# DeltaNet heads: decay rows broadcast from memory, key lengths from the Gram diagonal, one product for the output's squares, and no last state

## The chip, the cores and the metric

The kernel runs on one core of one Trainium2 chip. Such a core has five engines that run side by side and meet at semaphores: TensorE (PE in the profile, with PEld for its weight loads), VectorE (DVE), ScalarE (ACT), GpSimd (POOL) and SyncE (SP), which here only issues DMAs. The metric is the device time of one execution in microseconds. The kernel before took 3912.97 us (median of 3 runs, 3911.88 to 3916.1).

## The reference

The program is a network of four layers on 512 tokens of width 1024, with a context of 256 tokens. The change touches one mixer, the bidirectional gated DeltaNet. For each of 8 heads of width 128, and for each of two directions:

```
q, k, v = silu(conv3(h @ w_in));  q = l2norm(q) * 128**-0.5;  k = l2norm(k)
beta = sigmoid(...);  g = -exp(a_log) * softplus(... + dt_bias)
gc    = cumsum(g) within a chunk
decay = exp(gc_i - gc_j) for j <= i, else 0
L     = tril(beta * k k^T * decay, -1)
[u|w] = solve(I + L, [beta v | beta exp(gc) k])
per chunk:  v_new = u - w @ S
            o     = (q exp(gc)) @ S + (q k^T * decay) @ v_new
            S     = S * exp(gc_last) + (k exp(gc_last - gc))^T @ v_new
out = (o_forward + o_backward) * rsqrt(mean(o^2) + 1e-6) * onorm * silu(z)
```

The context (2 chunks of 128 tokens here) is scanned first and gives no output; its last state starts the scan of the 4 latent chunks. The state after the last chunk is used by nothing.

## The kernel before, in words

The stage `DeltaHeads` (class at L2133) does the heads one after another. Tokens are cut in `NTA` = 6 chunks of 128 (two of context, four latent). `l` is the direction, 0 forward and 1 backward. Each engine runs an order written out by hand, in `tensor`, `scalar`, `vector`, `gpsimd` and `sync`; semaphores with one count per head (`PER`, `COUNTED`) join them. A head has two parts:

- The inverse (`tensor_invert`, `scalar_invert`, `vector_invert`) builds (I + L)^-1 in levels v = 1 to 6. Per level and direction, PE multiplies (`masked`, L2498), DVE masks the product (L2838), PE adds it in (`update`, L2517 and L2519), and DVE transposes the sum for the next level (L2844, L2848) while ACT copies it (L2698). PE's small products of 64 rows go between: the values turned after v = 1, the keys turned in v = 3.
- The scan (`tensor_scan` and the others) walks 6 steps of both directions. Per step: `z` (L2554), the right side `r` on DVE (L2874), `vn` (L2568), copied by ACT (L2742), the output's two products (L2582, L2586), the state's product (L2591) and its update on DVE (L2893). Between these PE projects the next head's q, k, v and gate (`three`, L588, products of rounded float32), and DVE and ACT convolve and activate them.

What the change touches:

- Decay rows. `decays` (L2402) makes each direction's row of gc, repeated over the 128 partitions, by 6 products of a broadcast column with a triangle of ones, into PSUM banks 6 and 7. ACT's `decay` (L2635) reads it: 6 Relu, an exponential of those, and an exponential of the row itself. For head h+1, direction 0's products stand in level 5 of head h's inverse and direction 1's behind step 0 of its scan.
- Key lengths. `gram` (L2416) makes k k^T per chunk in step 3, and then, from squares that ACT took of k (`square_k`), 6 products with a column of ones (L2427). DVE's `column_scales` (L2765) takes those sums at the end of step 3.
- Output norm. In the next head's inverse: ACT squares o (`square_o`), PE sums in 8 products of one column (`tensor_sums`, L2457 and L2458, behind level 3), ACT takes the root (`deviate_o`), DVE inverts it (`invert_root`, in level 4), PE spreads it over the partitions in 4 products (`tensor_spread`, L2465, behind level 4), and DVE multiplies (`norm_o`, L2829).
- The last step of a scan makes a state that nobody reads (L2884, L2591, L2893).

The weights of the next head are four DMAs on SP, issued when the last projection of the head before is done; ACT rounds them (`weight_high`, in levels 1 to 4) and POOL makes their low parts (`weights_low`, L582).

Of the kernel before, what the change touches and what calls it, by code (L numbers as in the profile page):

```python
# [27 lines left out]
P = 128  # L28
# [1923 lines left out]
G_MIX = G_LANE + 2 * LANE  # L1952
LEVELS = 7
# [3 lines left out]
class DeltaGates:  # L1957
# [3 lines left out]
    def __init__(self, core):  # L1961
        self.c = core
        self.n = core.slab(k_slab(core.d["w_in_a_2"][0], 4 * D, 4 * D + 32))
        self.rows, self.rows0 = core.shared("table_in", 48)
# [168 lines left out]
class DeltaHeads(Stage):  # L2133
# [13 lines left out]
    PER = {"slab": 64, "full": 6, "centre": 5, "conv": 5, "silu": 6, "square": 1, "coef": 1, "nk": 1,  # L2147
           "osq": 1, "ostd": 1, "oroot": 1, "weighed": 1, "mixed": 1, "values_out": 1, "keys_out": 1, "qk": 1,
           "tri": 2, "cross": 2, "side": 1, "scored": 1, "a": 12, "a_in": 10, "a_out": 14, "x": 12,
           "upd": 12, "z": 10, "r": 10, "vn": 12, "vn_out": 13, "vnd": 12, "su": 12, "s": 12, "o": 1,  # L2150
           "begun": 7, "grew": 5, "onorm": 2}


    COUNTED = {"rows": ("begun", (1, 2)), "gram": ("begun", (3,)), "lens": ("begun", (4,)), "qkp": ("begun", (5,)),
               "turned": ("begun", (6, 7)), "flat": ("grew", (1, 3)), "grown": ("grew", (2, 4)), "eg": ("grew", (5,)),
               "osum": ("onorm", (1,)), "ospread": ("onorm", (2,))}

    def __init__(self, core, gates):
# [11 lines left out]
        self.sums, self.inverse, self.nk, self.root = (v(G_COL + 72 + 6 * i, n) for i, n in enumerate((NTA, NTA, NTA, NT)))  # L2170
# [33 lines left out]
    def gpsimd(self, pool):  # L2204
        for h in range(DHEADS):
            if h == 0:
                self.weights_low(pool, 0)
            self.halve_decays(pool, h)
            self.pool_head(pool, h)
            if h + 1 < DHEADS:  # L2210
                self.weights_low(pool, h + 1)
        self.weigh_o(pool, DHEADS - 1)
# [9 lines left out]
    def pool_head(self, pool, h):  # L2222

        if h:
            self.wait(pool, h - 1, "o", 1)
            self.wait(pool, h - 1, "s", 12)
# [12 lines left out]
        if h:  # L2239
            self.weigh_o(pool, h - 1)  # L2240

# [57 lines left out]
    def sync(self, sp):  # L2299
# [15 lines left out]
    def tensor(self, pe):  # L2315
        self.project(pe, 0, 1, range(KD))
# [5 lines left out]
        self.decays(pe, 0, 0)  # L2322
        self.decays(pe, 0, 1)
# [6 lines left out]
        self.tensor_spread(pe, DHEADS - 1)  # L2330

    def vector(self, dve):
# [18 lines left out]
        for h in range(DHEADS):  # L2351
            self.vector_invert(dve, h)
            self.vector_scan(dve, h)
        self.invert_root(dve, DHEADS - 1)
        self.norm_o(dve, DHEADS - 1)

    def scalar(self, act):
# [8 lines left out]
        self.square_k(act, 0)  # L2366
        self.centre(act, 0, 4)
        self.silu(act, 0, 3)
        self.silu(act, 0, 4)
        self.gate(act, 0)  # L2370
# [31 lines left out]
    def decays(self, pe, h, l):  # L2402

        c = self.c
        if l == 1:
            self.wait(pe, h, "grown", 1)
        elif h:
            self.wait(pe, h - 1, "keys_out", 1)
        else:
            pe.wait_ge(self.cols, 1)  # L2410
        for t in range(NTA):
            ins = pe.matmul(c.pair(6, KEYS)[:, P * t:P * t + P], self.g_all[:, t, l, h:h + 1].to_broadcast([P, P]),
                            c.const(("cum_f", "cum_b")[l]), start=True, stop=True)
        ins.then_inc(self.s["begun"], 1)

    def gram(self, pe, h):  # L2416
# [3 lines left out]
        self.wait(pe, h, "grown", 2)  # L2420
# [3 lines left out]
        ins.then_inc(self.s["begun"], 1)  # L2424
        self.wait(pe, h, "square", 1)
        for t in range(NTA):
            ins = pe.matmul(c.ps[:, 7, TC + t:TC + t + 1], self.lane(0, L_L, NTA, P)[:, t, :],  # L2427
                            c.const("ones")[:, 0:1], start=True, stop=True)
# [22 lines left out]
    def tensor_sums(self, pe, h):  # L2451

        c = self.c
        self.wait(pe, h, "osq", 1)
        for t in range(NT):
            out, cols = c.ps[:, 5, TC + t:TC + t + 1], slice(P * t, P * t + P)
            pe.matmul(out, self.o_sq[:, cols], c.const("one_over_p")[:, 0:1], start=True, stop=False)  # L2457
            ins = pe.matmul(out, self.q_sq[:, cols], c.eps(4), start=False, stop=True)  # L2458
        ins.then_inc(self.s["onorm"], 1)

    def tensor_spread(self, pe, h):
        c = self.c
        self.wait(pe, h, "oroot", 1)
        for t in range(NT):
            ins = pe.matmul(c.ps[:, 5, P * t:P * t + P], self.root[:, t:t + 1].to_broadcast([P, P]),  # L2465
                            c.const("ident"), start=True, stop=True)
        ins.then_inc(self.s["onorm"], 1)

    def tensor_invert(self, pe, h):
# [13 lines left out]
        def masked(v, l):  # L2483
# [5 lines left out]
            elif h and l == 0:  # L2489
                self.wait(pe, h - 1, "s", 12)  # L2490
# [38 lines left out]
        for v in range(2, LEVELS):  # L2529
# [4 lines left out]
            if v == 5 and h + 1 < DHEADS:  # L2534
                self.decays(pe, h + 1, 0)
# [4 lines left out]
            if v == 4 and h:  # L2540
                self.tensor_spread(pe, h - 1)

    def tensor_scan(self, pe, h):
        c, s = self.c, self.s
        more = h + 1 < DHEADS
        for step in range(NTA):
# [27 lines left out]
            for l in range(2):  # L2574
# [13 lines left out]
                self.wait(pe, h, "vnd", i + 1)  # L2588
                if i == 0:
                    self.wait(pe, h, "keys_out", 1)  # L2590
                pe.matmul(c.ps[:, 2 * l, 2 * P:3 * P], self.kt[:, t, :], self.st(l, 3), start=True, stop=True)\  # L2591
                    .then_inc(s["su"], 1)
            if more:
                self.project(pe, h + 1, step, range(5, KD))
                if step == 0:
# [1297 lines left out]
```

## Time and profile before

| | |
|---|---|
| runs before, median (lowest, highest) | 3912.97 us (3911.88, 3916.1) |
| the profiled execution | 3914.16 us |
| its span | 3912.3 us |
| PE busy | 3454.4 us, 88% |
| DVE busy | 1812.2 us, 46% |
| ACT busy | 1110.1 us, 28% |
| POOL busy | 420.5 us, 11% |

The profiled execution's time holds its span and 1.9 us around it. The busy share of an engine is an average over all stages; what an instruction is worth is read in its own stage, from the timeline. A row of the timeline gives a start, how long the merged group lasted, its line and its tiles; a bracket behind it gives the engine's idle time before it and who ended it. One float32 product shows as two matmul records.

### The profile page before, as it was taken

Reading aid. Unit: us, or ns where it says so; the run is one execution under the profiler, and the core shown is the slowest. Engines: PE = TensorE matmul, PEld = TensorE weight load, DVE = VectorE, ACT = ScalarE, POOL = GpSimd, SP = SyncE. Lnnn points to the kernel's source line nnn. Section 1 sums busy time; section 2 is a strip of 40 time slices with the busy share of each in tenths; the row PEclk is TensorE's granted clock in tenths of the full one; section 3 lists DMA queues with packets and bytes.
Section 4 is the critical chain, followed back from the end, with each engine's and each line's share of the span. In section 5 each row is a group of like instructions: output and inputs, shape, how many; then the busy total and the mean of one; then the engine's idle time right before and its main releaser. Section 6 shows DMA issues by size and latency. Waiting matters only on the chain. (4 is left out here: it accounts for less than half of the span.)

```text
span 3912.3 us, 48632 instructions
## 1 busy us (share of the span) xinstructions
PE 3454.4 (88%) x18766; PEld 2323.2 (59%) x18766; DVE 1812.2 (46%) x2892; ACT 1110.1 (28%) x1849; POOL 420.5 (11%) x420
## 2 busy tenths in 40 slices
PE   8999899878999899887999998699987896998886
PEld 6756577754756677755888887444332674443332
DVE  6773777447865777435455445411111543111112
ACT  3051433223201433235544453211111322111112
POOL 1200000000300000002222320011111000111110
PEclk7999999988999899998999998799999897999998
DMA  6430355320622255310001001299997413999995
GB/s 220 172 109 22 107 173 172 114 108 22 247 108 86 86 172 172 109 26 23 23 23 45 23 23 46 98 414 392 424 415 300 167 45 118 417 402 415 398 391 218
DMA packets 222472, 689.48 MB, mean 176 GB/s; under 512 B 27699, under 2 KB 107699, under 8 KB 197076
## 3 DMA queue, kind: packets, MB, share of 16 engines
q1 hardware_dynamic: 192000, 648.17, 43.2%
q10 hardware_dynamic: 11572, 21.96, 1.5%
q0 software_dynamic: 18720, 16.84, 1.3%
q8 instruction: 126, 2.06, 0.2%
q14 instruction: 54, 0.44, 0.0%
HBM read 697.38 MB, written 40.89 MB: 189 GB/s over the span
## 5 line engine op out<-in xcount | busy, mean ns | idle before, releaser
L588 PE MATMUL psum<-work_rounded 128*128 128x512 f32 (+1 forms) x2224 | 815.4, 407 | 80.3 <-DVE work_rounded L582 30.3
L588 PE MATMUL psum<-work_rounded,ring_rounded 128*128 128x512 f32 (+1 forms) x1824 | 726.1, 398 | 0.0
L588 PEld LDWEIGHTS psum<-work_rounded 128*128 128x128 f32 x2224 | 428.7, 193 | 203.0 <-issue 93.9
L3434 PE MATMUL psum<-ring,fixed 128*64 128x512 f32 x1184 | 415.8, 657 | 96.1 <-DMA ring<-in_w 52.9
L577 ACT ACTIVATE work_rounded<-ring 128x1024 fp32r<-128x1024 f32 x204 | 214.6, 1057 | 950.7 <-PE psum L588 692.7
L588 PE MATMUL psum<-fixed_rounded,work_rounded 128*128 128x512 f32 (+1 forms) x1088 | 435.9, 401 | 0.0
L588 PEld LDWEIGHTS psum<-work_rounded,ring_rounded 128*128 128x128 f32 x1824 | 352.6, 193 | 81.1
L3589 DVE TENSOR_TENSOR work<-work,psum 64x512 f32<-64x512 f32 (+1 forms) x64 | 44.2, 691 | 701.9 <-ACT work L3519 547.3
L582 DVE TENSOR_TENSOR ring_rounded<-ring,work_rounded 128x1024 fp32r<-128x1024 f32 x189 | 230.1, 1220 | 283.0 <-ACT work_rounded L577 283.0
L3434 PEld LDWEIGHTS psum<-ring,fixed 128*64 128x64 f32 x1184 | 131.7, 150 | 333.0 <-issue 333.0
L362 DVE SCALAR_TENSOR_TENSOR work<-ring,fixed,work 128x512 f32<-128x512 f32 x364 | 300.5, 835 | 24.8 <-issue 0.9
L3434 PE MATMUL psum<-work,fixed 128*64 128x512 f32 x512 | 240.8, 626 | 0.0
L588 PE MATMUL psum<-ring_rounded 128*128 128x512 f32 (+1 forms) x768 | 238.5, 372 | 0.3 <-issue 0.3
L588 PEld LDWEIGHTS psum<-fixed_rounded,work_rounded 128*128 128x128 f32 x1088 | 210.7, 194 | 46.6 <-issue 2.6
L1274 DVE SCALAR_TENSOR_TENSOR work<-psum,fixed,work 128x511 f32<-128x511 f32 (+1 forms) x152 | 109.4, 720 | 142.1 <-ACT work L1356 108.2
L3519 ACT ACTIVATE work<-psum 64x512 f32<-64x512 f32 x53 | 31.3, 590 | 477.5 <-PE psum L3434 477.5
L3422 PE MATMUL psum<-ring,fixed 128*128 128x512 f32 x352 | 158.9, 611 | 1.8 <-DVE fixed L3581 1.8
L3343 POOL DMA_INDIRECT pair_rows<-work x66 | 66.7, 1011 | 809.0 <-DVE work L3605 663.8
L582 POOL TENSOR_TENSOR ring_rounded<-ring,ring_rounded 128x1024 fp32r<-128x1024 f32 x32 | 76.7, 2410 | 715.8 <-ACT ring_rounded L577 715.8
L588 PEld LDWEIGHTS psum<-ring_rounded 128*128 128x128 f32 x768 | 139.2, 189 | 21.1 <-issue 1.6
L582 POOL TENSOR_TENSOR ring_rounded<-ring,fixed_rounded 128x1024 fp32r<-128x1024 f32 x23 | 48.6, 2115 | 873.3 <-ACT fixed_rounded L577 873.3
L588 PE MATMUL psum<-fixed_rounded,ring_rounded 128*128 128x512 f32 (+1 forms) x384 | 137.0, 357 | 0.0
(396 smaller groups left out, 5159.7 us busy)
## 6 DMA issues: line engine op xcount, KB each, us to landing
ring<-in_w SPq DMA_DIRECT2D x128, 2048.0 KB, 17.3
work<-in_w SPq DMA_DIRECT2D x64, 2048.0 KB, 21.5
ring<-in_mod_w SPq DMA_DIRECT2D x24, 2048.0 KB, 9.0
ring<-in_ada_w SPq DMA_DIRECT2D x24, 2048.0 KB, 7.9
ring<-in_ffn_w_in SPq DMA_DIRECT2D x44, 1024.0 KB, 7.6
ring<-in_ffn_w_out SPq DMA_DIRECT2D x10, 2048.0 KB, 7.7
ring<-in_w_in_a SPq DMA_DIRECT2D x32, 512.0 KB, 6.6
ring<-in_hy_w_in SPq DMA_DIRECT2D x6, 2048.0 KB, 8.2
```

The costliest lines, as they stand in the source:

```text
L362: ins = dve.scalar_tensor_tensor(out=acc, in0=w[:, k, :], scalar=c.par(cond, k), in1=acc, op0=ALU.mult, op1=ALU.add)
L577: return act.activation(c.rounded(out), v, ACT.Copy)
L582: return eng.tensor_tensor(c.rounded(v), v, c.rounded(v_high), ALU.subtract)
L588: ins = pe.matmul(out, c.rounded(w), c.rounded(x), start=(start and i == 0), stop=(stop and i == 2))
L1274: dve.scalar_tensor_tensor(out=out[:, 1:n], in0=u[:, 0:n - 1], scalar=w0, in1=out[:, 1:n], op0=ALU.mult, op1=ALU.add)
L3343: pool.indirect_dma_start(self.c.d["pair_rows"], bass.IndirectOffsetOnAxis(ap=self.si[:, b:b + 1].bitcast(U32), axis=0), self.y_sb[:, b, : ...
L3422: ins = pe.matmul(c.ps[:, 2 + j, :], self.gt_sb[:, k, :], weights(o, j)[:, k, :], start=(k == 0), stop=(k == KD - 1))
L3434: ins = pe.matmul(c.ps[64 * j:64 * j + 64, 2, :], self.gt_sb[:, k, 0:64], weights(o, j)[:, k, :], start=(k == 0), stop=(k == KD - 1))
L3519: act.activation(self.s_sb[64:P, :].rearrange("p (k q) -> p k q", k=4), by_row(c.ps[0:64, 2, :]), ACT.Silu)\
L3589: dve.tensor_tensor(hh, s_sb, by_row(c.ps[rows, bank, :]), ALU.mult).then_inc(self.prod, 1)
```

## The change

- `decays` and its products go. Once, before head 0, PE transposes the table of all gc (96 columns) and ACT copies it out and writes it to DRAM (`keep_table`). SP then loads each direction's row, repeated over 128 partitions (`load_rows`, 384 KB), into one buffer in SBUF: direction 1 of a head when ACT is done with direction 0 (`grown` 1), direction 0 of the next head when it is done with direction 1 (`grown` 2). SP's weight DMAs of a head stand ahead of its direction 1. `decay` reads the buffer.
- `square_k` and the 6 products with ones go. `column_scales` multiplies the Gram product by the identity's halves and reduces.
- `square_q` takes a scale, POOL adds it to the squared output (`add_q`, ahead of its other work on a head), and one product of 512 columns sums and repeats it. DVE transposes the result (`turn_o`, in level 4), ACT takes the root of every 32nd column after its copies of level 4, and DVE inverts and spreads by a transposition (`invert_root`, now in level 5). `tensor_spread` goes.
- The last step makes no new state.

```
     def sync(self, sp):
...
+        def load_rows(h, l):
+            rows = self.table.rearrange("(t l) (b n) -> l b t n", l=2, n=P)[l, h]
+            sp.dma_start(self.rows_sb, rows.partition_broadcast(P)).then_inc(self.s["rows"], 16)
+
         for h in range(DHEADS):
             if h:
                 self.wait(sp, h - 1, "full", 6)
...
+            if h == 0:
+                sp.wait_ge(self.gates.rows, self.gates.rows0 + 64)
+                load_rows(0, 0)
+            self.wait(sp, h, "grown", 1)
+            load_rows(h, 1)
+            if h + 1 < DHEADS:
+                self.wait(sp, h, "grown", 2)
+                load_rows(h + 1, 0)
...
     def pool_head(self, pool, h):
         if h:
+            self.add_q(pool, h - 1)
             self.wait(pool, h - 1, "o", 1)
...
+    def add_q(self, pool, h):
+        self.wait(pool, h, "osq", 1)
+        pool.tensor_tensor(self.o_sq, self.o_sq, self.q_sq, ALU.add).then_inc(self.s["ofull"], 1)
...
     def tensor(self, pe):
-        self.decays(pe, 0, 0)
-        self.decays(pe, 0, 1)
+        pe.wait_ge(self.cols, 1)
+        pe.transpose(c.ps[0:96, 6, 0:P], c.view(G_GC, 96), c.const("ident")).then_inc(self.gates.turned, 1)
...
     def gram(self, pe, h):
-        self.wait(pe, h, "square", 1)
-        for t in range(NTA):
-            ins = pe.matmul(c.ps[:, 7, TC + t:TC + t + 1], self.lane(0, L_L, NTA, P)[:, t, :],
-                            c.const("ones")[:, 0:1], start=True, stop=True)
...
     def tensor_sums(self, pe, h):
+        self.wait(pe, h, "ofull", 1)
+        pe.matmul(c.ps[:, 5, :], c.const("one_over_p"), self.o_sq, start=True, stop=True).then_inc(self.s["osum"], 1)
...
     def tensor_scan(self, pe, h):
-                self.wait(pe, h, "vnd", i + 1)
                 if i == 0:
                     self.wait(pe, h, "keys_out", 1)
-                pe.matmul(c.ps[:, 2 * l, 2 * P:3 * P], self.kt[:, t, :], self.st(l, 3), start=True, stop=True)\
-                    .then_inc(s["su"], 1)
+                if step < NTA - 1:
+                    self.wait(pe, h, "vnd", i + 1)
+                    pe.matmul(c.ps[:, 2 * l, 2 * P:3 * P], self.kt[:, t, :], self.st(l, 3), start=True, stop=True)\
+                        .then_inc(s["su"], 1)
...
+    def keep_table(self, act):
+        act.wait_ge(self.gates.turned, 3)
+        act.activation(self.rows_sb[0:96, 0, :], self.c.ps[0:96, 6, 0:P], ACT.Copy).then_inc(self.cols, 1)
+        act.wait_ge(self.cols, 2)
+        act.dma_start(self.table.rearrange("a (b n) -> (a b) n", n=P), self.rows_sb[0:96, 0, :]).then_inc(self.gates.rows, 16)
...
     def column_scales(self, dve, h):
+        for half in self.halves():
+            dve.tensor_tensor(diagonal[half], g[half, :, half], self.ident()[half], ALU.mult)
+        dve.drain()
+        dve.tensor_reduce(self.sums, diagonal, AX.X, ALU.add)
+        dve.drain()
...
     def vector_invert(self, dve, h):
                 self.cross(dve, h, v - 1)
+            if v == 4 and h:
+                self.turn_o(dve, h - 1)
+            if v == WHOLE and h:
+                self.invert_root(dve, h - 1)
             for l in range(2):
                 turn(v, l)
```

The order of the instructions, before and now, at three places. PE, head 1's inverse, from the end of the sums (L2457, L2458) over levels 4 and 5, before:

```order
L2457 MATMUL psum<-fixed,work 128x1
L2458 MATMUL psum<-fixed,work 128x1
L2498 MATMUL psum<-work 64x64 x24
L2519 MATMUL psum<-work 64x64 x24
L2465 MATMUL psum<-fixed,work 128x128 x4
L2498 MATMUL psum<-work 64x64 x24
L2412 MATMUL psum<-fixed,work 128x128 x6
L2517 MATMUL psum<-work 64x64
```

The spread (L2465) and the next head's decay rows (L2412) stand between the levels' own products. The same place now (L2490 is `masked`, L2509 and L2511 `update`, L2459 the new sum):

```order
L2511 MATMUL psum<-work 64x64 x24
L2459 MATMUL psum<-work,fixed 128x512
L2490 MATMUL psum<-work 64x64 x24
L2511 MATMUL psum<-work 64x64 x24
L2490 MATMUL psum<-work 64x64 x24
L2509 MATMUL psum<-work 64x64
```

One product of 512 columns stands where eight of one column stood, and nothing between levels 4 and 5 or within level 5. DVE, levels 4 and 5 of the same inverse, before (L2838 masks, L2844 transposes):

```order
L2818 TENSOR_SCALAR work<-work 128x12
L2838 TENSOR_TENSOR work<-psum,work 128x384 x2
L2844 STREAM_TRANSPOSE work<-psum 128x384 x2
L2822 RECIPROCAL work<-work 128x4
L2838 TENSOR_TENSOR work<-psum,work 128x384 x2
L2848 TENSOR_TENSOR work<-work,psum 64x384 x2
```

Now (the lines of the mask and the level's transposition have moved, the names of the tiles tell them):

```order
L2813 TENSOR_SCALAR work<-work 128x12
L2839 TENSOR_TENSOR work<-psum,work 128x384 x2
L2817 STREAM_TRANSPOSE work<-psum 128x512
L2845 STREAM_TRANSPOSE work<-psum 128x384 x2
L2839 TENSOR_TENSOR work<-psum,work 128x384 x2
L2822 RECIPROCAL work<-work 128x16
L428 STREAM_TRANSPOSE work<-work 128x512
L2849 TENSOR_TENSOR work<-work,psum 64x384 x2
```

A transposition of 512 columns (L2817) has come in ahead of level 4's own, and the reciprocal with a spread (L428) ahead of level 5's last addition. DVE, the end of step 3 of head 0's scan and the start of step 4, before:

```order
L2893 SCALAR_TENSOR_TENSOR work<-work,psum 128x128 x2
L2768 TENSOR_SCALAR work<-psum 128x6
L2770 RECIPROCAL work<-work 128x6
L2772 TENSOR_TENSOR work<-work 128x12
L2782 TENSOR_TENSOR work<-work,psum 64x384 x2
L2874 SCALAR_TENSOR_TENSOR work<-psum,work 128x128 x2
```

Now (L2900 is the state's update, L2877 the right side of step 4):

```order
L2900 SCALAR_TENSOR_TENSOR work<-work,psum 128x128 x2
L2759 TENSOR_TENSOR work<-psum,work 64x384 x2
L2761 TENSOR_REDUCE work<-work 128x6
L2763 TENSOR_SCALAR work<-work 128x6
L2765 RECIPROCAL work<-work 128x6
L2767 TENSOR_TENSOR work<-work 128x12
L2777 TENSOR_TENSOR work<-work,psum 64x384 x2
L2877 SCALAR_TENSOR_TENSOR work<-psum,work 128x128 x2
```

Three instructions of up to 384 columns have come in between the state of step 3 and the right side of step 4.

## Rows read from the trace of the kernel before

**Rows 1.** All heads: us, busy (x) of PE, PEld, DVE, ACT, POOL; clock, DMA share, GB/s

```profile
1838.00:2426.00 588.00, 556.99 (x6965) 494.51 (x6966) 298.45 (x689) 272.76 (x578) 148.83 (x99) 0.98 0.11 30
```

**Rows 2.** Timeline of TensorE: start, us, engine, line, operation, records, idle before

```profile
1926.61 0.38 PE L2457 MATMUL psum<-fixed,work 128*128 128x1 f32 x2
...
1932.45 1.16 PE L2465 MATMUL psum<-fixed,work 128*128 128x128 f32 x8 [0.77 <-DVEq L2823]
...
1933.54 1.61 PE L2498 MATMUL psum<-work 64*64 64x64 f32 x48
...
1935.09 1.60 PE L2412 MATMUL psum<-fixed,work 128*128 128x128 f32 x12
...
1949.57 1.60 PE L2412 MATMUL psum<-fixed,work 128*128 128x128 f32 x12 [0.29 <-ACT work L2645]
...
1951.01 0.61 PE L2554 MATMUL psum<-work 128*128 128x128 f32 x4
```

**Rows 3.** The same timeline, TensorE, later steps of head 1's scan

```profile
1960.46 0.39 PE L2586 MATMUL psum<-work 128*128 128x128 f32 x2
...
1966.62 1.40 PE L2427 MATMUL psum<-fixed,work 128*128 128x1 f32 x12
...
1973.30 0.75 PE L2568 MATMUL psum<-work 128*128 128x128 f32 x4
...
1988.56 0.86 PE L2480 MATMUL psum<-work,fixed 64*64 64x384 f32 x4 [0.26 <-DVEq L2798]
```

**Rows 4.** Timelines of ACT, DVE and TensorE, last projection to first inverse

```profile
1813.36 0.60 ACT L2623 ACTIVATE work<-psum 128x512 f32<-128x512 f32 x1 [1.98 <-PE psum L588]
...
1833.35 1.12 DVE L2782 TENSOR_TENSOR work<-work,psum 64x384 f32<-64x384 f32 x2
...
1838.08 1.55 PE L2480 MATMUL psum<-work,fixed 64*64 64x384 f32 x4 [5.61 <-DVEq L2798]
```

**Rows 5.** Timeline of ACT, next head's decay work in the scan

```profile
1944.97 1.66 ACT L2641 ACTIVATE work<-psum,work 128x128 f32<-128x128 f32 x6
...
1948.72 0.79 ACT L2645 ACTIVATE work<-psum 128x768 f32<-128x768 f32 x1
...
1953.68 1.67 ACT L2641 ACTIVATE work<-psum,work 128x128 f32<-128x128 f32 x6
...
1956.85 0.21 ACT L2648 ACTIVATE work<-work 128x12 f32<-128x12 f32 x1
```

**Rows 6.** DMA issues over the whole span: count, KB each, median us to landing

```profile
ring<-in_w_in_a SPq DMA_DIRECT2D x32, 512.0 KB, 6.6
...
work<-in_masks ACTq DMA_DIRECT2D x1, 416.0 KB, 3.9
```

**Rows 7.** Timeline of DVE, steps 3 to 5 of the scan

```profile
1970.84 0.16 DVE L2768 TENSOR_SCALAR work<-psum 128x6 f32<-128x6 f32 x1
...
1971.70 1.12 DVE L2782 TENSOR_TENSOR work<-work,psum 64x384 f32<-64x384 f32 x2 [0.19 <-issue]
...
1972.89 0.61 DVE L2874 SCALAR_TENSOR_TENSOR work<-psum,work 128x128 f32<-128x128 f32 x2
...
1986.50 0.55 DVE L2793 TENSOR_TENSOR work<-work 128x384 f32<-128x384 f32 x1
```

**Rows 8.** Timelines of ACT and POOL: next head's first weights, and a triangle

```profile
1922.54 1.06 ACT L577 ACTIVATE ring_rounded<-ring 128x1024 fp32r<-128x1024 f32 x1 [1.53 <-DMA ring<-in_w_in_a]
...
1923.68 4.68 POOL L582 TENSOR_TENSOR ring_rounded<-ring,ring_rounded 128x1024 fp32r<-128x1024 f32 x2 [3.11 <-ACT ring_rounded L577]
...
1956.33 1.84 POOL L2220 TENSOR_TENSOR work<-work,fixed 128x768 f32<-128x768 f32 x1 [5.63 <-ACT work L2644]
```

**Rows 9.** Timeline of DVE, head 1's triangular inverse

```profile
1927.24 1.22 DVE L2815 COPY work<-work 128x6 f32<-128x6 f32 x2
...
1929.45 1.26 DVE L2838 TENSOR_TENSOR work<-psum,work 128x384 f32<-128x384 f32 x2 [0.85 <-PE psum L2498]
```

**Rows 10.** One line's instructions (L428, a spread over 512 columns): min/median/max ns

```profile
L428 DVE STREAM_TRANSPOSE work<-work x15: 445/711/712, 52.1 to 3902.7; 128x512 f32<-128x512 f32 x13, 128x256 f32<-128x256 f32 x2
```

More of the change, by code:

```diff
@@ L2169, in __init__ @@
         self.kd, self.gl, self.eg, self.bg, self.coef, self.ahead = (v(G_COL + 12 * i, 2, NTA) for i in range(6))
-        self.sums, self.inverse, self.nk, self.root = (v(G_COL + 72 + 6 * i, n) for i, n in enumerate((NTA, NTA, NTA, NT)))
+        self.sums, self.inverse, self.nk, self.root = (v(G_COL + 72 + 6 * i, n) for i, n in enumerate((NTA, NTA, NTA, T // 32)))
+        self.rows_sb = v(G_ROWS, NTA, P)
+        self.table = core.d["h_rows"][0:2 * NTA, :]
         self.taps = v(PAR0 + PAR["conv_a0"][0], 3, 3, DHEADS)
@@ L2419, in gram @@
         self.wait(pe, h, "silu", 2)
-        self.wait(pe, h, "grown", 2)
+        if h == 0:
+            pe.wait_ge(self.cols, 2)
         for t in range(NTA):
@@ L2629, in convolve @@
             .then_inc(self.s["conv"], 1)
-    def square_k(self, act, h):
-        act.drain()
-        act.activation(self.lane(0, L_L, KEYS), self.k, ACT.Square).then_inc(self.s["square"], 1)
+    def keep_table(self, act):
[3 more added lines that the diff above has]
+        act.dma_start(self.table.rearrange("a (b n) -> (a b) n", n=P), self.rows_sb[0:96, 0, :]).then_inc(self.gates.rows, 16)
     def decay(self, act, h, l):
         c, s = self.c, self.s
-        m, rows = self.lane(l, L_M, NTA, P), c.pair(6, KEYS).rearrange("p (t n) -> p t n", n=P)
-        self.wait(act, h, "rows", l + 1)
+        m, rows = self.lane(l, L_M, NTA, P), self.rows_sb
+        self.wait(act, h, "rows", 16 * l + 16)
         for t in range(NTA):
@@ L2685, in deviate_o @@
         c = self.c
-        self.wait(act, h, "osum", 1)
-        act.activation(self.root, c.ps[:, 5, TC:TC + NT], ACT.Sqrt, bias=c.eps(5)).then_inc(self.s["ostd"], 1)
+        self.wait(act, h, "oturn", 1)
+        act.activation(self.root, fine(self.o_sq), ACT.Sqrt, bias=c.eps(5)).then_inc(self.s["ostd"], 1)
     def scalar_invert(self, act, h):
@@ L2818, in scan_columns, with turn_o @@
         dve.tensor_scalar(self.bg, self.eg, -1.0, None, ALU.mult)
+    def turn_o(self, dve, h):
+        self.wait(dve, h, "osum", 1)
+        dve.transpose(self.o_sq, self.c.ps[:, 5, :])
+        dve.drain().then_inc(self.s["oturn"], 1)
     def invert_root(self, dve, h):
@@ L2822, in invert_root @@
         dve.reciprocal(self.root, self.root)
-        dve.drain().then_inc(self.s["oroot"], 1)
+        dve.drain()
+        spread(dve, self.o_sq, self.root)
+        dve.drain()
     def norm_o(self, dve, h):
-        self.wait(dve, h, "ospread", 1)
         self.wait(dve, h, "weighed", 1)
-        dve.scalar_tensor_tensor(out=self.mixed(h), in0=self.mixed(h), scalar=self.c.par("onorm_a"), in1=self.c.ps[:, 5, :],
+        dve.scalar_tensor_tensor(out=self.mixed(h), in0=self.mixed(h), scalar=self.c.par("onorm_a"), in1=self.o_sq,
                                  op0=ALU.mult, op1=ALU.mult).then_inc(self.s["mixed"], 1)
@@ L2890, in vector_scan @@
                 t = self.order[l][step]
+                if step == NTA - 1:
+                    continue
                 self.wait(dve, h, "su", i + 1)
```

77 lines of the change are left out of this document (24 added, 53 removed).

## The prediction

> **What bounds the kernel now.** I read the busy time over the eight heads first [rows 1]: in 588 us PE is busy for 557, 95%, at a granted clock of 0.98, while DVE has 298, ACT 273 and POOL 149. So PE's own order sets the pace, and an instruction taken out of it is worth its time, unless PE would then stand at a wait that it covered. The timeline of PE shows where those are. From the first product of head 0's inverse at 1838.08 to that of head 2 at 1988.56 [rows 3, 4] two heads take 150.5 us, and the later ones repeat head 1. Within a head PE idles 0.3 to 0.8 us at a few places only, each with a bracket. The reader is to look there for who is late, and at the start of the stage, where PE idled 5.61 us before the first inverse [rows 4]. Then I read DVE, ACT and POOL beside PE, for what they do in the moment when PE would come earlier.
>
> **Step 0 of the scan: 1.73 us less.** The second set of decay rows starts at 1949.57 after 0.29 us of idleness and the next product starts at 1951.01 [rows 2]. Both go: 1.44 + 0.29 = 1.73. The state it needs next has been ready since before.
>
> That holds if the row load is in time, and this is the step with a new wait. ACT has finished direction 0 at 1948.72 + 0.79 = 1949.51 [rows 5]; SP issues the load then, and ACT stands before direction 1 until it has landed. Queued behind are the rest of `decay`, the copies of step 2's `vn`, and with them PE's second output product of step 2 (L2586) and the state's product. From the start of direction 1 to the end of its work ACT needs 1956.85 + 0.21 - 1953.68 = 3.4 us, and the copy 0.4 more [rows 5]. PE now comes to L2586 at 1960.46 - 1.73 = 1958.7 [rows 3]. So the load has 1958.7 - 3.8 - 1949.5 = 5.4 us; I take 5.3, since the state's product needs a DVE step too. The load is 384 KB to 128 partitions in runs of 512 bytes. Nearest rows: 416 KB of masks landed in 3.9 us, issued last of three; 512 KB of weights, in the same runs, in 6.6, as one of four issued together [rows 6], so its figure holds the queueing. I take 4.0; ends 2.6 (a third below the masks, for a queue with nothing ahead) and 6.6. At 4.0 nothing waits; at 6.6 it is 1.3 us in each of 7 heads, 9 in all.
>
> By the Trainium skill, DMA: Bandwidth & Descriptors, section "Anatomy of one DMA", a DMA takes about 2.0 us plus its bytes over 436 GB/s, an estimate of 2.9 us here. By that rule the sum would be some 2 us better than mine at the start of the stage and no different in the scan. The masks' row is a microsecond above it, and I keep the row.
>
> **Steps 3 and 4: 0.5 us more.** The sums of the squared keys are 12 records from 1966.62 on, 1.40 us with the tail of the last, 1.3 of PE's time [rows 3]. They go. But their sums come back on DVE, in front of step 4's right side: two products of 64x384 like L2782 (1.12 for two), a reduction over 384 columns (about 0.55, as one of these), and drains between (0.1): 1.8 [rows 7]. Has DVE room? The right side starts at 1972.89 in two halves of 0.3, and PE starts the `vn` that reads it at 1973.30 [rows 3, 7]: no slack at all. So PE stands 1.8 where it saved 1.3. ACT's square of the keys goes too, beside other work, at nothing.
>
> **Step 5: 0.45 us less** on PE: two products of the state, 4 records, at 12 records in 1.44 us [rows 2] 0.48. DVE loses its two updates and could begin the next inverse about 1 us ahead of 1986.50 (the products' 0.5 and two halves of 0.3, as the like right side takes [rows 7]).
>
> The scan in total: 1.73 - 0.5 + 0.45 = 1.7 us a head.
>
> **The inverse to level 5: 2.2 us less.** Here PE loses 8 sums (16 records, about 1.9 us) and gets one product of 512 columns (0.9, as 8 records of 128 columns by the same 1.44 for 12), and loses the spread with its wait: 0.77 and then 1.1 until 1933.54 [rows 2]. The boundary before could give 1 us more, since DVE is late there. That would be some 4 us. I don't count so much, as DVE is next late, held by something that the change doesn't move. ACT waits for the weights of the next head until 1922.54, SP having issued them with the end of the projections; POOL's first two low parts run from 1923.68 to 1928.36 [rows 8]; and DVE's tiny copies of 6 columns (1.22 us for two, from 1927.24 [rows 9]) end only when POOL is done. They are tied to the landing of the weights, however early PE is. Now from there: DVE masks level 4 at once, from 1928.6 rather than 1929.45, for 1.26 us [rows 9]; then the new transposition of the output's sums, 0.71 by the spread of as many columns [rows 10], with a drain 0.8; it ends at 1930.7. Level 4's own first transposition, of 384 columns, follows, 0.6 by the same row, and PE begins level 5 at 1931.3 instead of 1933.54: 2.2 less. Without the new transposition it would be near 3. The bounds: 1.3 if DVE's waits grow by another such step, 4.0 if POOL does not hold DVE. ACT's root comes later than now but before DVE asks for it.
>
> POOL's new addition is 1.2 us long, half of a low part with twice its columns [rows 8], and it waits for ACT's square, which stands behind two ACT copies of its size (0.60 each [rows 4]). So all of POOL's work on the head comes about 3 us later, up to the point where it waits for the weights anyway; that gap, 3.11 us [rows 8], covers it. What reads that work (step 1 of the scan and later, the low parts) is 10 us off.
>
> The Trainium skill, SBUF — State Buffer, section "Who interferes with whom", says that a DVE instruction with two inputs in SBUF and a GpSimd instruction that reads SBUF keep each other out, and so do DVE copies in a fast mode. It speaks against the change, which gives POOL an addition and `norm_o` a second input in SBUF. The copies above agree with it; were POOL's low parts pushed later, DVE would be held longer, a microsecond a head, inside my bounds.
>
> **Level 5: 1.44 us less.** The first decay rows start at 1935.09 [rows 2] and their 12 records take 1.44 as in step 0; DVE's mask is ready by then. The reciprocal and the spread, about 1.0 with drains [rows 10], now stand ahead of DVE's last addition. Between DVE's mask and that addition PE has 36 records for one direction, 1.2 us at 48 in the 1.55 from 1933.54 on [rows 2], which hides them.
>
> **Head 0, head 7, start, tail.** Head 0 has no output before it: 1.7 + 1.4 = 3.1. Head 7 has no weights to follow, so nothing holds DVE: about 2.2 + 1.0, and 0.5 in its scan: 3.7, the tail costing 0.1 (POOL's addition, a transposition and a spread for eight sums, a PE spread and its wait). The start: ACT is at the last projection's result at 1813.36 [rows 4]. PE's transposition and ACT's copy 0.6, the write out 2.6 (the low end again, 48 KB), a load 4.0: ACT begins at 1820.6. Direction 0, with a table load, is 1949.51 - 1944.97 = 4.5; the second load 4.0; direction 1's first exponential is there 1956.85 - 1953.68 - 0.7 = 2.5 later, at 1831.6; POOL's triangle 1.84 [rows 5, 8]. So DVE begins its second weighing at 1833.4, where it began at 1833.35 before [rows 4], and the first inverse follows as before, at 1838.1. The long waits are paid by the Gram products, the lengths, the scores and the first weighing, which ran behind the decays and now run beside the loads. I take 0, at ends -5 (6.6 us a load) and +3.
>
> **Sum.** Six heads at 1.7 + 2.2 + 1.44 = 5.34: 32.0; with 3.1, 3.7 and 0: 38.8. Against the profiled execution (3914.2; its span 3912.3 and 1.9 around) it gives 3875.4; it stood 1.2 above the median of the runs, so 3874.
>
> **The rivals.**
> - The loads are slow, 6.6 us: 9 us in the scans and 5 at the start come back, 3888. For it: the same short runs as the weights; against: nothing is queued ahead. 15 in 100.
> - The cover is gone: PE's removed work stood where it would wait anyway, for ACT's or DVE's copies, in level 5 and in step 0 as well. Half of the sum, 3894. For it: a chain of three engines in each level; against: in level 5 and step 0 the records follow without a gap. 12 in 100.
> - POOL does not hold DVE: the inverse gives 4.0 rather than 2.2, 6 times 1.8 is 11: 3863. 13 in 100.
> - Slower: 128 partitions that all read the same 3 KB of memory are served one after another. Each us of a load beyond 5.3 costs 7 in the scans, each beyond 4.0 costs 2 at the start: 7 (x - 5.3) + 2 (x - 4.0) = 38.8 gives x = 9.3 us, from which on the change loses. At twice the weights' figure, 13.2 us, it is 55 + 18 = 73 against 39: 3947. The trace shows no load of this kind of that size. 6 in 100.
>
> **How the numbers follow.** The forecast of 3874, with an own range of 3866 to 3884, has 54 in 100. Within 0.2% (8 us, what a measurement of this kernel can't tell from no change) lies only what is left between the half sum and the slow loads. Faster 91, same 3, slower 6. The range takes in the first three cases: 3861 to 3895.
>
> **What would show it.** Right: ACT's first Relu of direction 1 waits for a DMA of about 4 us and L2586's successor doesn't wait for ACT; PE idles about 1.8 us before `vn` of step 4 for DVE; level 5 starts at 0.5 us of idleness behind level 4; the two heads of 150.5 us take 142 (3.1 and 5.3 less); PE's first inverse starts near 1838. Wrong: a load over 5.3 us, with PE waiting for ACT in step 2, the two heads over 147 us, or PE waiting for DVE's inverse where it did not before.

## The result, and the profile after

| | before | after |
|---|---|---|
| median (lowest, highest) | 3914.53 us (3911.88, 3916.28), on the same chip | 3954.74 us (3950.0, 3956.11) |
| after / before | | 1.0102 [1.0089, 1.0115] |
| the profiled execution, its span | 3914.16, 3912.3 | 3950.0, 3948.2 |
| first products of head 1 to head 7, a sixth | 76.33 | 79.67 |

The change makes the kernel slower by 1.0%, 40 us, where 39 us less were forecast. The heads of the profile after, and three stretches of head 1 (the columns are those of [rows 1]):

```profile
1848.00:2444.00 596.00, 510.64 (x6438) 443.99 (x6439) 313.23 (x674) 265.16 (x561) 156.05 (x107) 0.94 0.18 42
1971.90:1978.30 6.40, 0.20 (x2) 0.01 (x1) 0.00 (x0) 3.79 (x11) 1.01 (x1) 0.72 0.06 14
1978.30:1985.00 6.70, 6.56 (x20) 5.40 (x21) 2.51 (x6) 2.85 (x6) 0.80 (x1) 0.50 0.19 37
1985.00:1988.00 3.00, 3.00 (x28) 3.00 (x27) 1.37 (x5) 1.20 (x3) 0.00 (x0) 1.00 0.22 44
```

PE was busy for 557 of 588 us [rows 1]; now it is for 511 of 596. The work is gone, the time is not: PE stands. The next two stretches show where. For 6.4 us in the middle of the scan it does nothing, and for the 6.7 us after that it is busy, but at a granted clock of 0.50, its lower level of 1.2 GHz.

Who is late is read from the row loads: the DMA's issues, what the loads took from issue to landing, and the waits over the heads (total us, times, longest).

```profile
work<-h_rows SPq DMA_DIRECT2D x16, 384.0 KB, 11.1
...
h_rows<-work ACTq DMA_DIRECT2D x1, 48.0 KB, 1.5
```

```profile
DMA to landing us min/median/max: 10.9/11.1/12.5
```

```profile
ACT work L2630 <- DMA work<-h_rows: 78.4, 8, 12.6
...
PE psum L2574 <- ACT work L2733: 45.6, 7, 7.4
...
PE psum L2472 <- DVEq L2793: 37.8, 2, 37.5
...
PE psum L2490 <- DVE work L2845: 16.2, 22, 0.9
...
PE psum L2556 <- DVE work L2877: 11.8, 7, 1.7
```

A load takes 11.1 us in the median and never under 10.9, where 4.0 were taken. ACT stands for it before direction 1 of each head (L2630 is `decay`'s Relu), the copy of `vn` (L2733) stands behind it, and PE's second output product of step 2 (L2574, L2586 before) waits 45.6 us in seven heads. The timelines of PE and of ACT in head 1 show it as one event:

```profile
1971.72 0.38 PE L2570 MATMUL psum<-work 128*128 128x128 f32 x2
...
1978.37 0.80 PE L2574 MATMUL psum<-work 128*128 128x128 f32 x2 [6.26 <-ACT work L2733]
...
1984.95 0.63 PE L2542 MATMUL psum<-work 128*128 128x128 f32 x4
```

```profile
1974.44 1.86 ACT L2630 ACTIVATE work<-work 128x128 f32<-128x128 f32 x6 [9.15 <-DMA work<-h_rows]
...
1977.96 0.61 ACT L2733 ACTIVATE work<-psum,work 128x128 f32<-128x128 f32 x2
```

From L2574 to the next `z` (L2542) 6.58 us pass. The same instructions took 3.22 before, from 1960.46 [rows 3] to `z` at 1963.68. So the stall costs 6.3 us and the slower stretch behind it another 3.4. At the start of the stage two such loads follow each other, and the first inverse begins 40.6 us after PE ends its last projection (at 1807.91), where it was 24.8 (from 1813.32 to 1838.08):

```profile
1838.23 1.86 ACT L2630 ACTIVATE work<-work 128x128 f32<-128x128 f32 x6 [12.57 <-DMA work<-h_rows]
```

```profile
1848.47 1.55 PE L2472 MATMUL psum<-work,fixed 64*64 64x384 f32 x4 [37.52 <-DVEq L2793]
```

From that projection to the last head's `norm_o` the two profiled executions differ by 40.2 us: the start +15.8, head 0 +6.9, heads 1 to 6 +20.0, head 7 -2.5. (Their spans differ by 35.9 only, mainly since the projection itself ends 5.4 us earlier in the profile after (1807.91 against 1813.32); how long the part ahead of the stage takes changes by some us from one execution to the next.)

### The profile page after: what moved, and what is told of

It reads as the page before. It is cut to its first block and busy times, and to the rows that moved or that the text cites. A ratio compares the mean times of both kernels' runs of the same rounds, so it can differ in the third digit from the quotient of the medians.

```text
span 3948.2 us, 47684 instructions
## 1 busy us (share of the span) xinstructions
PE 3409.1 (86%) x18271; PEld 2274.2 (58%) x18271; DVE 1832.9 (46%) x2900; ACT 1106.9 (28%) x1842; POOL 429.3 (11%) x428
## 5 line engine op out<-in xcount | busy, mean ns | idle before, releaser
L362 DVE SCALAR_TENSOR_TENSOR work<-ring,fixed,work 128x512 f32<-128x512 f32 x364 | 302.3, 840 | 24.8 <-issue 0.9
```

Of the source, the lines that this page charges most:

```text
L362: ins = dve.scalar_tensor_tensor(out=acc, in0=w[:, k, :], scalar=c.par(cond, k), in1=acc, op0=ALU.mult, op1=ALU.add)
```

## The experiments

Theory A at the outset: the removed work is worth what was forecast, and the load's 11 us took it away. The rivals: the loads are no cause, the added work on DVE and POOL is (B); and, for why a load is slow, its many short runs (C), its one address for all partitions (D), or its pieces 8 KB apart (E). The tables of the decays are in memory 2048 numbers apart, so that a row repeated over 128 partitions is 6 pieces of 512 bytes, 8 KB apart. Ratios are to the kernel before on the same chip. The letters in the expectations below are each run's own.

**e1_other_rows.** The same size and runs, but each partition reads an address of its own, in a weight. It leaves out the right decays: they are made from a weight's numbers, so other tokens are routed to the experts later, and its whole time says nothing. The pieces of the weight's rows lie 1 KB apart rather than 8, so address and distance both change.

```
-rows = self.table.rearrange("(t l) (b n) -> l b t n", l=2, n=P)[l, h]
-sp.dma_start(self.rows_sb, rows.partition_broadcast(P))
+rows = c.d["w_in_a_2"][0][0:P, 0:2 * KEYS].rearrange("p (t x n) -> x p t n", x=2, n=P)[0]
+sp.dma_start(self.rows_sb, rows)
```

> The changed kernel with one edit: each row load reads 128 different rows of a weight tensor in the same runs of 512 bytes and the same shape (128 x 6 x 128), instead of one row of the table 128 times. So the decays are made from other numbers. In the changed kernel a load took 11.1 us to land. Theory A (one address): the 128 partitions read the same 3 KB of memory and are served one after another; then a load here lands in about 4 us, PE's stall in step 2 (6.26 us) goes and the time falls to about 3875 to 3885. Theory B (shape): the load is slow for its form, since few of the 16 DMA engines work on it (the DMA share in a load was 0.2); then it lands in 11 us here too and the time stays at about 3950.

The load landed in 3.5 us. The data queue's row in the window of one load, of the kernel after and then of this one, gives packets, MB and the share of the 16 engines:

```profile
q1 hardware_dynamic: 784, 0.39, 17.9%
```

```profile
q1 hardware_dynamic: 784, 0.39, 40.9%
```

The same 784 packets, so not their number (C falls). Whether the address or the distance did it, this run alone can't say.

**e2_runs.** The table is written so that a row is one run of 3 KB, in one place for all partitions. For this ACT issues six DMAs instead of one.

```
+for t in range(NTA):
+    act.dma_start(self.runs()[:, P * t:P * t + P], self.rows_sb[16 * t:16 * t + 16, 0, :])
...
+sp.dma_start(self.rows_sb.rearrange("p t n -> p (t n)"), self.runs()[DHEADS * l + h].partition_broadcast(P))
```

> The changed kernel with the table written so that the row of one head and direction is one run of 3 KB; a load still repeats it over 128 partitions, from one address, but in 128 runs of 3 KB instead of 768 of 512 bytes. Theory A (one address serialises by bytes): 11 us to land as before, time about 3950. Theory B (shape: the six pieces leave few engines, or cost per piece): about 4 us to land, no stall of PE in step 2, the clock stays full in the scan, and the start is 14 us shorter: 7 heads x (6.3 stall + 3.2 lost to the halved clock behind it) + 14 = 80 us less than 3954, so about 3874.

3872.43 us (3870.77 to 3874.66), 0.9893 [0.9878, 0.9908]. The load landed in 3.4 us with one address, so D alone falls too. The waits of ACT and of PE's first inverse; PE's for the copy of `vn` (45.6 us after) is not among this kernel's waits any more:

```profile
PE psum L2472 <- DVEq L2797: 23.2, 2, 23.0
...
ACT work L2634 <- DMA work<-h_rows: 12.4, 8, 3.3
```

Nothing else of the change was touched, and the time is within 2 us of the forecast. A holds, and B falls as the cause of the loss. PE's wait for DVE behind the Gram diagonal is still there, 1.68 us in each of seven heads and two shorter ones:

```profile
PE psum L2556 <- DVE work L2881: 12.1, 9, 1.7
```

Yet the granted clock stays at its upper level, 2.4 GHz, over the heads. The columns are those of [rows 1]:

```profile
1842.00:2360.00 518.00, 482.45 (x6377) 423.38 (x6373) 304.99 (x659) 264.39 (x558) 154.15 (x105) 1.00 0.16 44
```

**e5_pitch_1k, e6_pitch_8k_other, e10_pitch_4k, e11_pitch_8k_pad** (one execution each). Pieces of 512 bytes in all of them. e5: one address, pieces 1 KB apart. e6: 8 KB apart, an address for each partition (it too leaves out the right decays, taking a weight's numbers). e10: one address, 4 KB apart. e11: one address, 8.5 KB apart. The core of the edits:

```
e5   .rearrange("(x t y n) -> y x t n", t=NTA, y=2, n=P)[0]
e6   bass.AP(tensor=flat.tensor, offset=flat.offset, ap=[[P, P], [2048, NTA], [1, P]])
e10  bass.AP(tensor=flat.tensor, offset=flat.offset, ap=[[6144, 16], [1024, NTA], [1, P]])
e11  bass.AP(tensor=flat.tensor, offset=flat.offset, ap=[[128, 16], [2176, NTA], [1, P]])
```

> The changed kernel with the table's pieces of one row 1 KB apart in memory instead of 8 KB: each load still reads one address for all 128 partitions, in 768 runs of 512 bytes. So far a load of the same form took 11.1 us from one address with pieces 8 KB apart, 3.5 us from 128 addresses with pieces 1 KB apart, and 3.4 us from one address in whole runs of 3 KB. Theory A (the six pieces 8 KB apart fall on one part of the memory, and all partitions hit it): 3.5 us to land here, time about 3873. Theory B (many short reads of one and the same 512 bytes are slow whatever lies between): 11 us, about 3950.

> The changed kernel with each load from a weight tensor, pieces 8 KB apart as in the table, but each partition 512 bytes further on, so 128 addresses per piece. The decays are made from other numbers. Theory A in its plain form (8 KB between pieces is enough to be slow): 11 us to land. Theory A in its full form (8 KB between pieces and one address for all): about 3.5 us. Theory B (one address): 3.5 us. With e5_pitch_1k this tells the three apart. Its total time is not to be compared, since other numbers may choose other experts later.

> The changed kernel with the pieces of a row 4 KB apart in memory (8 KB: 11.1 us to land, 1 KB: 3.5 us). One address for all partitions, 768 runs of 512 bytes. Theory: the pieces meet in one part of the memory if the distance is a large power of two. If 4 KB is large enough too, it is 11 us, and the time about 3950; if two parts share the load, 6 us, about 3890 to 3900; if not, 3.5 us and 3873.

> The changed kernel with the pieces of a row 8.5 KB apart (8 KB and 512 bytes of padding) instead of 8 KB. Theory: what is slow is the distance of exactly 8 KB; then the padding gives 3.5 us to land and a time of about 3873, as the smallest mend of the changed kernel. Rival: any distance of some KB is slow with one address for all, then 11 us and 3950.

| | addresses | pieces apart | landing us | time us |
|---|---|---|---|---|
| after | one | 8 KB | 11.1 | 3954.74 |
| e10 | one | 4 KB | 6.7 | 3906.32 |
| e11 | one | 8.5 KB | 3.5 | 3871.93 |
| e5 | one | 1 KB | 3.5 | 3873.53 |
| e2 | one | one run | 3.4 | 3872.43 |
| e6 | 128 | 8 KB | 3.5 | (3838.24) |
| e1 | 128 | 1 KB | 3.5 | (3836.59) |

It takes both: one address for all partitions and pieces 4 or 8 KB apart. Half a kilobyte more between the pieces gives the whole load back. e10 and e11 write the table in the same way, so the writing is not the cause. That it is large powers of two that are slow is a guess from these distances; others, such as 12 KB, were not tried. The transfer has no slow end; in the window of one load (40 slices of 0.28 us) the kernel after and e1 move, in GB/s:

```profile
GB/s 0 0 0 5 45 43 43 40 45 43 45 40 45 42 47 40 43 43 47 38 45 43 33 9 45 43 43 42 43 45 43 40 42 47 45 40 24 15 63 0
```

```profile
GB/s 0 0 0 0 0 0 0 0 0 0 0 0 100 144 138 138 166 161 138 155 161 277 338 338 354 338 327 277 233 205 127 78 50 11 0 0 0 0 0 0
```

A steady 43 GB/s against up to 354 (e1's slices are 0.09 us). That fits pieces that all meet in one part of the memory and are served in turn; what part that is, no run here shows. By the Trainium skill, DMA: Bandwidth & Descriptors, section "Latency and other measured facts", copies whose partitions' rows lie 4 or 8 megabytes apart fall to half their rate, and a few kilobytes of padding restore it. The kind agrees; here it takes only 4 to 8 KB, where many partitions read one address, and 512 bytes of padding were enough.

e10 also shows that a short stall can be dear; its time is 6 us above the 3890 to 3900 expected for such a load. The load is late by some 2 us, and the timeline of PE in head 1 has:

```profile
1961.61 0.38 PE L2569 MATMUL psum<-work 128*128 128x128 f32 x2
...
1963.82 0.49 PE L2573 MATMUL psum<-work 128*128 128x128 f32 x2 [1.83 <-ACT work L2737]
...
1969.38 0.61 PE L2541 MATMUL psum<-work 128*128 128x128 f32 x4
```

The stretch behind the stall is 5.56 us rather than 3.22 (another wait of 0.38 us is in it), and the row of its window, with a clock of 0.83, names the main reason:

```profile
1960.00:1970.00 10.00, 7.79 (x35) 6.50 (x34) 2.71 (x7) 6.54 (x15) 1.80 (x1) 0.83 0.31 39
```

The heads take 74.09 us where 70.5 is the figure without a stall. Waits of 1.1 to 1.95 us cost 3.6 a head. It is not so in every head. Behind the five waits of 1.55 to 1.95 us the stretch up to the next `z` has a mean clock of 0.68 to 0.69 and lasts 5.3 to 5.6 us. Behind those of 1.34 and 1.12 us (from 2112.71 and 2335.09 on) the clock is 1.00 and the stretch 4.0. And in e2 PE idles 1.68 us for the diagonal in every head at a clock of 1.00. So the length of the wait alone does not settle whether the clock falls behind it.

**e3_two_buffers.** The loads stay slow but get a buffer for each direction, so that a row is loaded a whole head before it is read.

```
+self.row_bufs = [v(slots[3] + 512 + KEYS * l, NTA, P) for l in range(2)]
...
+if h + 1 < DHEADS:
+    for l in range(2):
+        self.wait(sp, h, "grown", l + 1)
+        load_rows(h + 1, l)
```

> The changed kernel with two row buffers, one for each direction, in a part of the weight ring that is idle there; a buffer is loaded for the next head as soon as ACT has read it for this one, one head ahead. The loads themselves are as slow as before (11 us). Theory: the whole loss is the wait for the load; it goes in 7 heads, with PE's stall (6.3 us a head) and the halved clock behind it (3.2 us a head), 67 us, and at the start the second load no longer waits for the first direction, 6 to 12 us. So about 3876 to 3882 against 3954, a head takes 70 to 71 us instead of 79.7, and my sum for PE's removed work (39 us less than before) is right but for the start. Rival: the loss is elsewhere (the new work on DVE and POOL), and the time stays over 3914.

3880.9 us (3875.71 to 3883.99), 0.9913 [0.9899, 0.9926], with loads of 11.3 us. In the heads a slow load costs nothing once no engine stands for it: 70.52 us a head, as e2. What it still costs against e2, 8 us in all, lies for the most part ahead of head 1's first product, which is 7 us later in the profile (1914.69 against 1907.72): 3.0 before the first inverse and 3.4 in head 0.

**e4_lengths_back, e7_best, e9_state_back, e8_norm_back** size the other parts. e4 is e3 with the key lengths from ACT's squares and products with ones, as before. e7 joins the best of all: runs of 3 KB, two buffers, lengths as before. e9 is e7 with the last state made again, e8 is e7 with the output's norm as before (8 products, a spread, no work of POOL's). Their edits, each in a line or two:

```
e4, e7  +self.square_k(act, h + 1)                                  # in step 2 of the scan
        +dve.tensor_scalar(self.sums, self.c.ps[:, 7, TC:TC + NTA], RMS_EPS, None, ALU.add)
e9      -if step < NTA - 1:
        +if True:
e8      -pe.matmul(c.ps[:, 5, :], c.const("one_over_p"), self.o_sq, start=True, stop=True)
        +pe.matmul(out, self.o_sq[:, cols], c.const("one_over_p")[:, 0:1], start=True, stop=False)
        +pe.matmul(out, self.q_sq[:, cols], c.eps(4), start=False, stop=True)
```

> As e3_two_buffers, with the key lengths made as in the kernel before: ACT squares k, PE makes 6 products with a column of ones, and the Gram diagonal's three DVE instructions go. By my term for steps 3 and 4 the diagonal costs 0.5 us a head net (1.8 us of PE waiting for DVE, 1.3 us of PE saved), so this is 4 us faster than e3_two_buffers in 7 heads, and PE's wait before vn of step 4 is gone. Rival: PE's 1.3 us count and the wait hides elsewhere, then it is up to 9 us slower than e3_two_buffers.

> What the runs so far point to, together: the table written in runs of 3 KB, two row buffers loaded one head ahead, key lengths by products with ones as in the kernel before, and the rest of the change. Heads as in e4_lengths_back (70.1 us each), and the start shorter than in e2_runs by one load of 3.4 us, since both directions load at once: 3872.4 - 3.9 for the lengths - 3.5 = about 3865. If the start is bound by something else, 3869.

> e7_best with the state after the last step made again, as in the kernel before. By my terms it costs PE 0.45 us a head, since the rest of the gain at the boundary is lost to the wait of DVE's copies for POOL: 7 x 0.45 + 0.5 = about 4 us over e7_best. Rival: the chain over DVE at the boundary counts in full, 1.2 to 1.7 us a head: 8 to 12 us over.

> e7_best with the output norm as in the kernel before: sums in 8 products of one column behind level 3, the root in level 3 on ACT, the spread in 4 products behind level 4; no addition on POOL, no transpositions of 512 columns on DVE. By my term the new norm is worth most of 2.2 us a head in 7 inverses: 15 us over e7_best. Rival: without the new DVE and POOL work the old form loses less, since DVE's collisions with POOL go (1.6 us for one instruction in level 1, PE waiting 0.9): then 8 us over.

> e7_best once more, beside e8_norm_back on the same chip, so that the two can be subtracted: within 3 us of e7_best's time in the run before.

| | time us (lowest, highest) | ratio | a head, 1 to 6 |
|---|---|---|---|
| e4 | 3877.01 (3875.63, 3879.61) | 0.9906 [0.989, 0.9921] | 70.15 |
| e7 | 3866.56 (3862.02, 3867.59) | 0.9883 [0.9866, 0.99] | 70.15 |
| e7_again (e7 once more, beside e8) | 3869.44 (3868.48, 3877.98) | 0.9895 [0.988, 0.991] | 70.07 |
| e9 | 3875.6 (3872.82, 3877.63) | 0.9907 [0.9889, 0.9924] | 70.59 |
| e8 | 3882.94 (3881.05, 3886.36) | 0.9923 [0.991, 0.9937] | 72.23 |

The period of a head is the sharper measure, since whole times of two programs differ by a few us from ahead of the heads: e7's first inverse began at 1830.76 in one profile and at 1836.54 in the other. By it the diagonal costs 0.37 us a head (e3 less e4), the last state 0.44 (e9 less e7), the norm 2.08 to 2.16 (e8 less e7 and less e7_again). Between e9 and e7 the whole times differ by 9.0, which taken alone would fit the rival's 8 to 12. But of this the heads explain 4.4 (545.0 us against 549.4 from the first product to the last `norm_o`); the rest lies ahead of them and is no part of the state's price. e8 is 13.5 above e7_again, where 15 were expected and the rival had 8. The heads of e7, in the columns of [rows 1], have PE busy for 94.5% at a clock of 0.99:

```profile
1830.80:2375.00 544.20, 514.31 (x6592) 450.69 (x6592) 303.97 (x673) 275.49 (x578) 158.71 (x109) 0.99 0.15 43
```

e7 is the best version by its parts: 1.2% faster than before (1.1% in e7_again) and 2.2% faster than after. The whole times don't part it from e2, whose ratio of 0.9893 lies inside both intervals. In the profiles it leads e2 by 0.37 us in each of heads 1 to 6, and by 3.3 at the start: from the last projection's end to the first inverse 22.7 us pass rather than 26.0, since the two loads no longer follow each other.

## Why the prediction was wrong

| term of the sum, us | forecast | measured | by |
|---|---|---|---|
| all of a head's parts, no stall | 5.34 | 5.81 | e2 |
| key lengths | +0.5 | +0.37 | e3, e4 |
| last state | -0.45 | -0.44 | e9, e7 |
| inverse to level 5 | -2.2 | -2.3; the norm alone -2.1 | before, after; e8, e7 |
| decay rows (level 5 and step 0) | -3.17 | -3.4 | before, after |
| head 0, no stall | -3.1 | -3.8 | e2 |
| head 7 | -3.7 | -2.5; -1.1 | after; e2 |
| a load's landing | 4.0, ends 2.6 and 6.6 | 11.1 | after |
| its price in a head | 0 | 9.1 | after, e2 |
| start | 0, between -3 and +5 | +15.8; +1.3 | after; e2 |

The measured parts of a head close: 2.3 + 3.4 + 0.44 - 0.37 = 5.8. The first is the time from a head's first product to level 5 (head 1: 21.23 us before, 18.89 after), the second that from there to the scan's first `z` (17.47 and 14.05). That e2's whole time meets the forecast within 2 us is in part luck: head 7 and the start fell short by 3.9 us, and the other heads gave 3.5 more.

**The step that failed** is "I take 4.0; ends 2.6 and 6.6". Both ends came from loads that give each partition rows of its own. The prediction had the slower case as its last rival, "128 partitions that all read the same 3 KB of memory are served one after another", with its price from x = 9.3 us on, and gave it 6 in 100. It came true in that the change loses; in its cause only by half, since one address is harmless when the pieces do not lie 4 or 8 KB apart (e2, e5, e11). The stride of the table, which the change's own lines give, was never put beside the address; the masks and the weights [rows 6] bound the size and the length of the runs, not this.

**The rival's price was too low as well.** With x = 11.1 its formula gives 7 x 5.8 + 2 x 7.1 = 55 us against the 42 that e2 saves: 13 us slower, where 40 were measured. PE's waits in the seven heads are 45.6 us, near the formula's 41. (In each head the wait was the load's time less 5.0, not 5.3, since PE came earlier, and some loads took over 12 us.) But behind each of these waits the granted clock is at its lower level for a time: from L2574 to L2542 the seven heads of after took 5.27, 6.58, 5.30, 5.08, 6.41, 5.16 and 5.15 us rather than 3.22 each, 16.4 us in all. No term spoke of the clock. In heads 1 to 6 the sum closes to within 1 us: 6 x 5.81 = 34.9 less, 40 of waits and 14.4 of clock more, against +20 measured.

**The start.** Two loads, of 10.9 and 12.5 us instead of 4.0 each, are 15.4 of the 15.8. Head 0 was to give 3.1 and takes 6.9 more. Its stall and the clock are 8.4 of these 10. For the rest SP has this row:

```profile
1842.16 13.44 SPq L2324 DMA_DIRECT2D ring<-in_w_in_a  x4
```

Head 1's weights are issued at 1842.16, behind the loads, and queue behind the last one: ACT waits for them until 1861.39 and POOL's first low parts hold DVE's small copies, here 2.16 us for two; PE waits 1.78 us behind them. The prediction asked who waits behind the loads on ACT, but not for the weights on SP's queue.

By the Trainium skill, DMA: Bandwidth & Descriptors, section "Anatomy of one DMA", the 2.0 us plus the bytes over 436 GB/s that the prediction quotes is a fit for DMAs of the gpsimd path. SP's loads here took 3.4 to 3.5 us with a harmless pattern (e2, e5, e11), not the estimate of 2.9.

**What held.** DVE comes 1.67 us late to step 4 behind the diagonal (1.8 forecast; the wait of L2556 on L2877 above). The write out is short, 1.5 us. Behind level 4 PE waits 0.27 us, forecast 0.5:

```profile
1946.99 0.70 DVE L2817 STREAM_TRANSPOSE work<-psum 128x512 f32<-128x512 f32 x1
1947.82 1.05 DVE L2845 STREAM_TRANSPOSE work<-psum 128x384 f32<-128x384 f32 x2
```

```profile
1948.46 1.61 PE L2490 MATMUL psum<-work 64*64 64x64 f32 x48 [0.27 <-DVE work L2845]
```

The transposition of the sums and the level's own follow each other as worked out. The rival "the cover is gone" falls with it: the whole sum came.

**Right in size, wrong in reason: the inverse's 2.2.** The prediction took 2.2 rather than 4.0 because POOL's low parts hold DVE's small copies, tied to the weights' landing. In heads 1 to 6 the traces don't bear that out. In the kernel before, the first copy took 1.14 us in head 1 and 0.13 in head 6, and level 5 began 21.23 us behind the head's first product in both. In the kernel after, it took 0.60 to 1.43 us in heads 1, 2, 4, 5 and 6 and level 5 began at 18.89 in all five; only in head 3, where it took 1.66, was level 5 later, by 0.16. So the condition of the rival "POOL does not hold DVE" came true where it counts, and its 4.0 did not come. What stands in the way is DVE's own chain, which the prediction left out. The boundary gave the microsecond that it named (level 1's second group of products starts 2.01 us into the head, not 3.12), but PE loses 0.94 of it at level 2, where it had not waited before (a sign of being wrong that the prediction had named):

```profile
1935.78 1.61 PE L2490 MATMUL psum<-work 64*64 64x64 f32 x48 [0.94 <-DVE work L2845]
```

**Head 7 and the tail.** Head 7 was to give 3.7 and gave 2.5, by the same error. It was to have a microsecond more in its inverse, since no weights follow to hold DVE. But it gave 2.16 there (21.52 us to level 5 before, 19.36 after), no more than the others, and 0.33 in its scan. The tail, priced at 0.1, came out even: from the scan's last product to the end of `norm_o` 6.9 us pass in both kernels, though PE now waits there for POOL's addition:

```profile
2458.30 1.13 PE L2459 MATMUL psum<-work,fixed 128*128 128x512 f32 x2 [2.71 <-POOL work L2249]
```

In e2 the same product runs at a clock of 0.50 and takes 2.07 us, and the tail is 0.9 us longer, part of why head 7 gave only 1.1 there.

## What to carry to other kernels

A DMA that repeats memory over partitions is priced by its address pattern, not by its size and run length alone: lay what is repeated out as one run, or pad its pieces off the distance that is slow (here 8 KB and 4 KB), and measure it before an engine stands for it. Where such a load has slack, a second buffer hides even a slow one (e3). And a stall of the bounding TensorE can cost more than its length, for the clock that follows it: 1.4 times in after (16.4 us behind waits of 45.6), twice and more in five heads of e10, but once only behind the 1.68 us of e2. Read the granted clock behind each stall before you price it.

## What the runs showed of the hardware that was not expected

- One address for 128 partitions with pieces 8 KB apart: 11.1 us for 384 KB; 4 KB apart 6.7; 8.5 KB, 1 KB or no gap 3.4 to 3.5.
- The clock at 0.50 behind a stall of 6.3 us for 6.7 us, and 2.3 us more behind one of 1.8, a wait of 0.4 among them; but the clock at 1.00 throughout the heads of e2, with a wait of 1.68 us in each.
- POOL's addition, ahead of its other work, moved that work some 2.5 us further into the inverse, beside another DVE instruction with two inputs in SBUF. Timelines of DVE and POOL of the kernel after, head 1:

```profile
1933.60 1.63 DVE L2803 SCALAR_TENSOR_TENSOR work<-work 64x384 f32<-64x384 f32 x1
...
1938.67 0.57 DVE L2803 SCALAR_TENSOR_TENSOR work<-work 64x384 f32<-64x384 f32 x1
```

```profile
1932.54 0.83 POOL L2235 COPY work<-work 128x768 f32<-128x768 f32 x1
...
1933.54 2.81 POOL L2238 TENSOR_TENSOR work<-work 128x512 f32<-128x512 f32 x2 [0.18 <-issue]
```

The first of the two equal DVE instructions takes 1.63 us and the second 0.57; before, all 16 took 0.55 to 0.56. But before, another one (L2795, 0.56 us alone) took 1.15 in heads 1 to 7, in head 1 beside POOL's copy, and takes 0.56 in those heads now. It cost PE little: PE waits 0.94 us there, but as long behind the short one as well, and 0.87 at the same place in e8, which has no addition on POOL. By the Trainium skill, SBUF — State Buffer, section "Who interferes with whom", a DVE instruction with two inputs in SBUF and a GpSimd instruction that reads SBUF contend. This row agrees, with 1.1 us.
